# A hybrid attention block on one core: queries, keys and three gate blocks projected in token form, word planes split by GpSimd

## What is computed

```python
h = rms_norm(x, norm_gain)
proj = jnp.einsum('btd,de->bte', h, w_in)
qa, ka, va, ga, qb, kb, vb, gb, qi, ki, wi = jnp.split(proj, offsets, axis=-1)
out_a = chunked_relpos_attention(heads(qa), heads(ka), heads(va), rel_bias)
out_b = dsa_sparse_attention(heads(qb), heads(kb), heads(vb), qi, ki, wi, slopes)
y = jnp.concatenate([out_a * silu(ga), out_b * silu(gb)], axis=-1)
x = x + jnp.einsum('bte,ed->btd', y, w_out)
return rms_norm(x, final_gain)
```

## Time and profile before

| | us |
|---|---|
| median of 3 runs | 521.59 |
| lowest and highest | 521.50, 522.29 |
| the profiled execution's own time | 520.91 |
| its span, first to last instruction | 518.8 |
| PE, PEld, DVE, ACT, POOL busy | 509.6, 442.2, 364.7, 306.1, 31.1 |

### The profile page before, as it was taken

The page is one execution under the profiler, slowest core; times in us unless marked ns, Lnnn a source line. Parts: engine busy times, 40 slices in busy tenths (PEclk is TensorE's granted clock), DMA queues, the critical chain, the costliest instruction groups (busy, mean ns, idle before and its releaser), DMA issues.

```text
span 518.8 us, 7543 instructions
## 1 busy us (share of the span) xinstructions
PE 509.6 (98%) x2736; PEld 442.2 (85%) x2736; DVE 364.7 (70%) x544; ACT 306.1 (59%) x415; POOL 31.1 (6%) x47
## 2 busy tenths in 40 slices
PE   8999999999999999999999999999999999999994
PEld 6989999888888888888888888888888878888883
DVE  5798776775856787867776776687878778646554
ACT  6876555446564554445675849495868676544342
POOL 1000054140400000000000000000000000000000
PEclk9999999999999999999999999999999999999999
DMA  8984787758795776553956575665647875576614
GB/s 276 356 261 134 241 262 257 245 176 244 230 271 163 251 215 222 179 190 99 284 145 228 158 228 167 190 192 163 198 159 231 288 230 171 195 207 200 198 42 162
DMA packets 83933, 107.79 MB, mean 208 GB/s; under 512 B 26400, under 2 KB 68288, under 8 KB 83648
## 3 DMA queue, kind: packets, MB, share of 16 engines
q1 hardware_dynamic: 82320, 101.92, 63.3%
q0 software_dynamic: 1296, 5.01, 3.0%
q10 hardware_dynamic: 288, 0.46, 0.2%
HBM read 99.24 MB, written 2.11 MB: 195 GB/s over the span
## 4 chain that ended last, share of the span: by engine, by line
PE 97%; DMA 1%; DVE 0%; issue 0%; ACT 0%; DVEq 0%; POOLq 0%
PE acc L506 28%; PE acc L475 14%; PE acc L477 14%; PE acc L476 14%; PE acc L510 14%; PE acc L526 4%; PE acc L534 3%; PE aux L536 2%; PE aux L658 1%; PE aux L667 1%; DMA gain<-norm_gain 1%; PE aux L655 0%; PE aux L656 0%; PE aux L673 0%; PE aux L654 0%; PE aux L672 0%
## 5 line engine op out<-in xcount | busy, mean ns | idle before, releaser
L1068 DVE TENSOR_TENSOR lo_slots<-raw_slots,hi_slots 128x1024 fp32r<-128x1024 f32 x166 | 204.7, 1240 | 105.1 <-ACT hi_slots L735 103.8
L735 ACT ACTIVATE hi_slots<-raw_slots 128x1024 fp32r<-128x1024 f32 x166 | 174.3, 1056 | 140.7 <-PE acc L477 91.3
L506 PE MATMUL acc<-acts,hi_slots 128*128 128x512 f32 (+1 forms) x640 | 195.5, 387 | 0.0
L510 PEld LDWEIGHTS acc<-acts,lo_slots 128*128 128x128 f32 x640 | 119.3, 188 | 22.7
L475 PE MATMUL acc<-hi_slots,acts 128*128 128x512 f32 x320 | 124.9, 390 | 0.7 <-issue 0.7
L476 PE MATMUL acc<-lo_slots,acts 128*128 128x512 f32 x320 | 124.6, 389 | 0.0
L477 PE MATMUL acc<-hi_slots,acts 128*128 128x512 f32 x320 | 124.5, 389 | 0.0
L510 PE MATMUL acc<-acts,lo_slots 128*128 128x256 f32 (+1 forms) x640 | 123.8, 275 | 0.0
L506 PEld LDWEIGHTS acc<-acts,hi_slots 128*128 128x128 f32 x640 | 97.4, 189 | 0.1
L475 PEld LDWEIGHTS acc<-hi_slots,acts 128*128 128x128 f32 x320 | 60.1, 188 | 13.0 <-issue 0.9
L477 PEld LDWEIGHTS acc<-hi_slots,acts 128*128 128x128 f32 x320 | 60.1, 188 | 12.6
(11 more groups left out here) (179 smaller groups left out, 478.0 us busy)
## 6 DMA issues: line engine op xcount, KB each, us to landing
raw_slots<-w_blocks SPq DMA_DIRECT2D x140, 512.0 KB, 4.4
raw_slots<-wo_blocks SPq DMA_DIRECT2D x32, 512.0 KB, 4.2
raw_slots<-w_blocks SPq DMA_DIRECT2D x8, 256.0 KB, 5.3
qk<-x POOLq DMA_DIRECT2D x1, 2048.0 KB, 10.7
qk<-xT SPq DMA_DIRECT2D x7, 256.0 KB, 5.3
o<-ext_dram POOLq DMA_DIRECT2D x1, 1024.0 KB, 10.0
fgain<-final_gain POOLq DMA_DIRECT2D x1, 1024.0 KB, 8.0
out<-o SPq DMA_DIRECT2D x2, 512.0 KB, 3.0
```

The lines of the kernel that those rows point to most:

```text
L506: nc.tensor.matmul(whole, w_hi4[:, u % RING, q, f * HD:f * HD + HD], acts[:, k, :, tokens], start=(k == 0), stop=False)
L510: last = nc.tensor.matmul(acc[:, bank:bank + n], w_lo4[:, u % RING, q, f * HD:f * HD + HD], a_hi[:, k, tokens], start=False, stop=(k == KT ...
L735: nc.scalar.activation(hi_slots[:, s, 0:UK * CB], w_raw[:, s, :], ACT.Copy).then_inc(hi_done, 1)
L1068: nc.vector.tensor_tensor(lo_slots[:, s, 0:UK * CB], w_raw[:, s, :], hi_slots[:, s, 0:UK * CB].bitcast(f32), ALU.subtract).then_inc(lo_don ...
```

## The change

Blocks 10 to 16, that is group A's queries and keys and three of the four gate blocks, are computed in token form. Each goes the way that blocks 4 to 7 went: `projection_out` on ACT, planes, DMA transpose, `join_projection` on ACT. The planes of these seven blocks, and those of all eight pairs' probabilities, are made by GpSimd. Only block 17 stays in feature form, with its two halves in the other pair of PSUM banks; the output blocks change banks as well. The features' low-half copies and additions are gone for blocks 10 to 16, and so is the multiplication by `rk`: the row scale is applied in `projection_out`. The tanh of a gate block is one instruction of 128 x 1024. In a pair's list the join and the pair's output now stand behind split 13, ahead of the next pair's exponentials. The turn of the probabilities moves behind the load of unit 2. In block 17 both halves of gate block 16 are applied too, and the first two `y_hi` and `y_lo` stand ahead of split 10 instead of behind it. `planes_made` is a new wait of the next pair's bias on DVE.

```diff
+            def split_projection(n):
+                pool.wait_ge(proj_out, n + 1)
+                nc.gpsimd.tensor_copy(proj_planes(n)[0], halves(z)).then_inc(proj_split, 1)
+                pool.wait_ge(proj_split, n + 1)
+            def split_planes(pair):
+                pool.wait_ge(normed, pair + 1)
+                nc.gpsimd.tensor_copy(planes, halves(probs)).then_inc(planes_made, 1)
+                pool.wait_ge(planes_made, pair + 1)
+            pool.wait_ge(qnow_ready, 8)
+            split_planes(0)
+            for n in range(N_LATE, N_END):
+                split_projection(n)
+                if n < N_END - 1:
+                    split_planes(n - N_LATE + 1)
             pool.wait_ge(scored, HEADS)
             pool.dma_start(x_flat.rearrange("p (m d) -> p m d", m=TM), x).then_inc(res_landed, 16)
+            split_planes(HEADS - 1)
...
             for pair in range(HEADS):
                 g = pair + G_QKA
-                pe.wait_ge(feat_out, 2 * g - 17)
-                feature_unit(g, 0)
...
+                if pair < 2:
+                    both_out(pair + 3)
+                else:
+                    pe.wait_ge(proj_out, pair + N_LATE - 1)
+                for u in range(UNITS):
+                    if g < G_OUT - 1:
+                        unit(g, u)
+                    else:
+                        if u == 4:
+                            pe.wait_ge(proj_out, N_END)
+                        feature_unit(g, u)
+                    if u == 0 and pair > 0:
+                        value_pair(pair - 1)
+                    if u == 1:
+                        pe.wait_ge(proj_joined, (4, 4, 4, 4, 7, 7, 8, 8)[pair])
+                        score_pair(pair, 2 * pair + 1 if pair < 4 else pair)
...
+            def pair_attention(g, pair, staged):
+                exps(pair, pair < 4)
                 split_hi(g, 6)
-                features_low(g, 0, 0)
-                planes_out(i)
                 split_hi(g, 7)
+                if pair > 4:
+                    tanh_gates(pair - 5)
                 split_hi(g, 8)
                 split_hi(g, 9)
+                stage_q(*staged)
+                pT_out(pair)
                 split_hi(g, 10)
-                features_low(g, 1, 0)
+                if pair > 4:
+                    act.wait_ge(y_done, 2 * (pair - 4))
+                projection_out(g)
                 split_hi(g, 11)
                 split_hi(g, 12)
-                output(i)
                 split_hi(g, 13)
+                join_projection(pair + N_LATE)
+                act.wait_ge(proj_joined, pair + N_LATE + 1)
+                output(pair)
```

More of the change, by code:

```diff
@@ L290, in halves, with proj_planes, proj_home @@
             return flat(words[:, :, :]).bitcast(u16).rearrange("p (n s) -> p s n", s=2)
-        proj_planes, proj_planes_T = (o_flat[:, n * T * 4:(n + 1) * T * 4].bitcast(u16).rearrange(
-            "p (s n) -> p s n", s=2) for n in range(2))
-        def proj_halves(chunk):
-            return qk[:, :, :].bitcast(u16).rearrange("p c (n s) -> p s c n", s=2)[:, :, chunk:chunk + 3:2, :]
+        PROJ_WORDS = 4 * T
+        def proj_planes(n):
+            if n < N_GATE:
+                at = D * (n >= N_LATE)
+                pair = (o_flat[:, at:at + PROJ_WORDS], o_flat[:, at + PROJ_WORDS:at + 2 * PROJ_WORDS])
+            else:
+                pair = (v1_flat[:, 0:PROJ_WORDS], o_flat[:, 3 * PROJ_WORDS:4 * PROJ_WORDS])
+            return [t.bitcast(u16).rearrange("p (s n) -> p s n", s=2) for t in pair]
+        def proj_home(n):
+            if n >= N_GATE:
+                return halves(z).rearrange("p s (c n) -> p s c n", c=2)
+            first, step = ((0, 2), (4, 2), (1, 2), (5, 2), (0, 1), (2, 1), (4, 1), (6, 1))[n]
+            return qk[:, :, :].bitcast(u16).rearrange("p c (n s) -> p s c n", s=2)[:, :, first:first + step + 1:step, :]
         def feature_use(g, half, early):
-            return 2 * g + (half - 2 * G_QI if early else half - 16)
+            return 2 * g + half - 2 * G_QI if early else EARLY_USES + half
         def narrow_loads(p):
@@ L498, in feature_unit @@
                 tokens = slice(start_token, T)
-                pair = half
+                pair = 1 - half if g == G_OUT - 1 else half
                 pe.wait_ge(lo_done, g * UNITS + (u + 1))
@@ L708, in _ @@
                 for u in range(UNITS):
-                    unit(g, u)
+                    unit(g, u, 1)
             g = G_END - 1
@@ L929, in exps @@
                 last.then_inc(exp_done, 1)
-            def planes_out(pair):
-                act.wait_ge(normed, pair + 1)
-                nc.scalar.activation(planes, halves(probs), ACT.Copy).then_inc(planes_made, 1)
             def pT_out(pair):
@@ L990, in _, with tanh_gates @@
-            with act.Fori(0, 3) as i:
-                g = i + G_GATE
-                gate_block(g, i, i + 1)
-                features_low(g, 1, 0)
-                split_hi(g, 11)
-                split_hi(g, 12)
-                tanh_gate(i, 1)
-                output(i + 4)
-                split_hi(g, 13)
+                join_projection(pair + N_LATE)
+                act.wait_ge(proj_joined, pair + N_LATE + 1)
+                output(pair)
+            def tanh_gates(i):
+                act.wait_ge(proj_joined, i + N_GATE + 1)
+                nc.scalar.activation(flat(t_gate[:, :, :]), flat(z[:, :, :]), ACT.Tanh, scale=0.5).then_inc(tanh_done, 1)
@@ L1001, in y_hi, with tanh_last @@
+            def tanh_last(half):
+                act.wait_ge(gate_rated, half + 1)
+                nc.scalar.activation(t_gate[:, half, :], z[:, half, :], ACT.Tanh, scale=0.5).then_inc(tanh_done, 1)
+            for pair, staged in enumerate(((2, 3, 4), (4, 5, 4), (6, 7, 4), (0, 4, 7), (1, 5, 7), (2, 6, 8), (3, 7, 8))):
+                pair_attention(pair + G_QKA, pair, staged)
             def y_hi(q):
@@ L1396, in bias_b @@
                 dve.wait_ge(scored, pair + 1)
+                if pair > 0:
+                    dve.wait_ge(planes_made, pair)
                 for t, (p, d, bank, n) in enumerate(((p1, dist1, aux[0], T), (p0, dist0, aux[1], P))):
@@ L1500, in y_lo @@
                                         a_hi[:, UK * q:UK * q + UK, :].bitcast(f32), ALU.subtract).then_inc(ylo_done, 1)
-            gate_block(G_OUT - 1, 3, False)
-            for q in range(4):
-                y_lo(q)
+            g = G_OUT - 1
+            probabilities(HEADS - 1)
+            split_lo(g, 6)
+            gated(2, 0)
+            gated(2, 1)
+            gate_out(0)
+            split_lo(g, 7)
+            gated(3, 0)
+            split_lo(g, 8)
+            split_lo(g, 9)
+            y_lo(0)
+            y_lo(1)
+            split_lo(G_OUT - 1, 10)
+            y_lo(2)
+            y_lo(3)
             pT_rest(HEADS - 1)
-            gate_out(G_OUT - 1, 3, 1)
+            gate_out(1)
             split_lo(G_OUT, 3)
```

211 lines of the change are left out of this document (80 added, 131 removed).

## The result

| | before | after |
|---|---|---|
| median, us | 521.62 (521.50 to 523.23, 6 runs) | 539.23 (536.86 to 540.03, 6 runs) |
| span of the profiled execution | 518.8 | 537.5 |
| POOL busy | 31.1 | 79.9 |

A forecast was written before the change was run, and what follows sets the result against it. PE, busy 98% of the span, was taken to bound the kernel. Profiled 520.91 - 3.5 (token form) + 1.2 (value pairs) + 3.8 (last gate block) = 522.4; with 0.7 for the median, 523.1 us, range 518 to 532.

The forecast's parts named there:

- The gain on PE: Blocks 10 to 16: token form streams faster, seven times 22.3 less 21.8, -3.5 us; pair period 24.1.
- The loop: Chain from one pair's normalise to the next through GpSimd, DMA, ACT and DVE: 24.15 us against a period of 24.1.
- Where GpSimd and DVE both work, they take turns: Planes copy behind normalise: waits for one DVE split, 1.15 us, then copies, 1.5, while DVE's next split waits.
- The copy's own price: GpSimd's one-input copies: 1.5 us for 1536 halfwords (planes), 2.0 for 2048 (projection).
- three of the rivals: On GpSimd's copies: fast or no exclusion, 518.1, chance 0.22; 0.9 ns pace, 521.4, 0.21; dearer, 530, 0.20.
- Dearer copies: Rival: GpSimd's copies take 2.0 and 2.65 us, the loop 25.3, the time 530; chance 0.20.
- the two-input price: Rival: GpSimd's copies cost 2.1 ns an element, 3.3 and 4.4 us; loop 28.3, time 551; chance 0.07.
- The fast case: Rival: copies as fast as DVE's, or not holding its splits; loop 22.7 or 23.0, time 518.1; chance 0.22.
- The value pairs: PE's wait for turned probabilities, one unit into the next block: 0.2 us for each of six, +1.2.
- every 0.1 us more in one step costs 0.7 us: Without slack in the loop, a longer step counts in each of the seven turns.
- The last gate block: PE stalls 3.0 us before unit 7 and 1.5 before block 18, less the earlier 0.69 wait: +3.8.
- The order on SP: Loads behind the turns come up to 2 us later, but land some 5 us before ACT may split them.

The follow-up runs named there:

- k9: k8 with its last gate block reordered again: ACT's join, tanh and low half ahead of split 7, DVE's split 7 behind the first gating; 517.76 us.
- k6: Changed kernel, with DVE waiting for GpSimd's planes between splits 6 and 7; 525.24 us.
- k10: Changed kernel, with DVE waiting between splits 6 and 7 for the end of its own split 6, not for GpSimd; 525.72 us.
- k1: Changed kernel, but ACT makes the planes of the probabilities behind split 6, GpSimd keeps the projections; 521.50 us.
- k8: Changed kernel with planes on ACT (k1), join and output later (k4, all seven), and the last gate block reordered; 522.49 us.
- k2: Changed kernel, with DVE waiting for GpSimd's planes ahead of split 6 in pairs 0 to 6; 534.99 us.
- k3: Changed kernel, but DVE makes the planes of the probabilities right behind normalise, GpSimd keeps the projections; 531.32 us.
- k4: Changed kernel, but ACT's join and output of a pair stand behind split 7 of the next pair, except for the last projection; 522.51 us.
- k7: Kernel before the change, with GpSimd also copying the planes of pairs 0 to 5 into unread memory, DVE waiting for it at the next bias; 521.29 us.
- k5: k3 with the turn of the planes ahead of the load of unit 2 in SP's queue; 521.57 us.
- k11: Changed kernel, GpSimd's planes kept, with their turn ahead of the load of unit 2 in SP's queue; 542.68 us.

## Why the prediction was wrong

**The gain on PE** was right: the value pairs of k9 come every 24.15 us instead of 24.62 (forecast 24.1), 3.3 us over seven blocks against 3.5. Its median is 3.65 us below that of the kernel before. Its profiled execution, the slowest of five, is only 1.4 us shorter in span, but PE was already 1.4 us behind in it within the first 20 us, with 0.7 us more of waits.

**The loop** was found, its members too, and eight of nine terms are right to 0.3 us. **The step that failed** is "Where GpSimd and DVE both work, they take turns". Its rows showed exclusion (rows 8: 0.82 and 1.70, 1.22 and 1.85), always with a single instruction of each. I read a fair exchange into it, and booked 1.15 + 1.5 for the planes: wait for one split, then copy, and let DVE's next split wait. The trace has 4.7 and in one round 6.8. Where the gap was given, in k6 and k10, the value pairs waited 0.2 and 0.5 us in all, and from the first to the seventh PE took 146.00 and 146.02 us, 1.0 more than in k9 (145.05), against 1.2 forecast. The time was 525.2 and 525.7; much of the 2 us above the forecast is the clock, which after the wait of 3.3 us in the last gate block was low there (PE lost 3.1 us in the profiled k6 and 1.7 in k10). The copy's own price, the unknown that got all the attention and three of the rivals, was right: 1.47 for 1.5, 1.90 for 2.0.

**The rivals.** Dearer copies (530, and 551 at the two-input price) had the right mechanism and the wrong cause; that case counted from 3.5 us for both copies together, behind the first split, and counted so they came to 5.5 (4.73 less 1.15, and 1.9). The range stopped at 532 because the 551 case was thought to need a price of 2.1 ns an element. A queue of DVE work wasn't seen as a price. The fast case (518.1) would have needed no exclusion; k9 reached that time by another way.

**The value pairs** were booked at 0.2 us each for six; seven waited 1.6 us each. By the sentence "every 0.1 us more in one step costs 0.7 us", 2.1 us more in one step would make 14.7; 11.2 were measured, and 1.4 of them are the first pair's, outside the loop. The sentence should have widened the range.

**The last gate block** was booked at 3.8 more, against 4.5 of waits less 0.7: right as a sum, by luck. 1.24 us were spent ahead of unit 6, where no wait was forecast, and none at the start of the output projection, where 1.5 more was booked; and normalise of pair 7 came later than forecast, since the turn of the last projection took 7.0 us instead of 4.35. Unit 7 was ready 7.5 us after normalise (436.10 less 428.63; forecast 8.0). In k1, with ACT's planes, it waits at the two places of the forecast, 1.85 and 1.25 us, and the step from k8 to k9 shows what the order of the block's instructions alone is worth, the clock included: 4.7 us.

**The clock** was missing: 4.9 us behind the two longest waits. A forecast with no wait above 0.2 us before the last gate block could leave it out there, but not behind its own stall of 3.0 us. That would still have been a matter of chance: a wait of 3.3 us was followed by the lower clock in k6 and k10, and not in k2.

**The order on SP** was called harmless ("the loads behind the turns come later, but land"). I asked what the turn does to the loads behind it, not what the load ahead, with its wait for split 6, does to the turn. Hidden in the changed kernel, it costs 2.8 us a round in k3.

## What to carry to other kernels

When a chain runs through several engines from one round to the next, compare its sum with the round's length before anything else: with no slack every term counts, and a step of slack (k4) gave back 16.7 us, nearly as much as taking the copy off GpSimd altogether (k1, 17.7). Where two engines exclude each other, ask not only for how long, but who is next while the other has work queued; a wait of the one engine for its own last instruction, or an instruction that reads PSUM, lets the other in. In a queue look both ways: at what a moved DMA delays, and at what the entry ahead of it waits for.

## What the runs showed of the hardware

- A GpSimd copy from SBUF to SBUF doesn't get in between DVE instructions with two SBUF operands that follow without a gap: it took 6.68 us beside six of them, 4.60 beside three, 3.46 beside two, 2.33 beside one, and 1.47 with DVE idle (k2). A gap of about 0.1 us is enough (k10), and so was a high half that became ready 0.08 us or less before DVE's next split.
- It runs beside a DVE instruction that has one operand in PSUM (k7).
- A one-input copy of halfwords on GpSimd took 1.47 us for 1536 and 1.90 for 2048 elements a partition, on DVE 0.96 and 1.22.
- A DMA transpose of 1536 halfwords took 3.7 us from issue to use, and 4.7 to 5.1 when a load of 512 KB had been issued 0.4 us ahead of it (k1, k2, k3).
- PE's granted clock fell to its lower level around the end of waits of 3.29 and 3.71 us, and was high again 6.2 and 4.2 us after PE had gone on. In other runs it fell after waits of 1.94 to 2.09 us (k4, k5, k11) and stayed high after one of 3.28 (k2).
